# Gate projections of a two-block fp32 transformer: sixteen groups of two tiles over ten pipeline steps, and a second branch with two tiles to a PSUM bank

## The chip, the cores and the metric

One core of one Trainium2 chip. The metric is the device time of one execution in microseconds (us), the median of three runs. One more execution was taken with the hardware profiler; its trace is what is read below.

## The reference

Two transformer blocks on 256 tokens of width 2048, one layer each, all in fp32. The change lies in the second block:

```python
proj = h @ w_in[layer]
qa, ka, va, qb, kb, vb, ga, gb = jnp.split(proj, IN_OFFSETS, axis=-1)
ya = sliding_window_attention(qa, ka, va, sink_logits) @ w_branch_a[layer]
yb = stick_breaking_attention(qb, kb, vb) @ w_branch_b[layer]
merged = jax.nn.sigmoid(ga) * ya + jax.nn.sigmoid(gb) * yb
x = x + merged @ w_out[layer]
x = x + swiglu(rmsnorm_2(x, norm_ffn_g[layer]), w_ffn_in[layer], w_ffn_down[layer])
```

`ga` and `gb` are 2048 columns wide each, so the gate projection is a [256 x 2048] by [2048 x 4096] product. Each attention has 16 heads of 64; its output is 1024 wide, and `w_branch_a`, `w_branch_b` take it to 2048.

## The kernel before

All products are in fp32 precision made of three fp32r products: a weight and an activation are each split in a rounded part `hi` and a rest `lo`, and hi*hi, hi*lo and lo*hi are added in PSUM. Features lie on the partitions, the 256 tokens (`T`) in the free dimension; an output tile is 128 features by 256 tokens, an input tile `kt` likewise. The block's activations stand in `pair[:, kt, 0]` (hi) and `pair[:, kt, 1]` (lo).

**Weights.** They stream from HBM in chunks of 128 x 1024 fp32 (512 KB) into six buffers `raw`. For each chunk ScalarE (ACT) copies it, rounded, into `hi` (L383), VectorE (DVE) writes the rest into `lo` (L396), and TensorE (PE) multiplies. `hi` and `lo` have four slots, so ACT may split chunk c only when PE has used chunk c-4 (`weights_used`). A chunk holds eight blocks of 128 x 128. Each engine works through its own list in the order written; semaphores tie them.

**Two forms of the product.** `features` (L436), the wide form: one matmul of `hi` with both parts of the activation (512 columns, into the two halves of a bank) and one of `lo` with the hi part (256 columns, into the second half). A whole bank holds one tile, and DVE adds the halves later (`sum_out`, L1264). `three` (L446) and the same written out at L2110 to L2114: three matmuls of 256 columns into one half of a bank, so two tiles fit in a bank and nothing is left to add.

**Attention pipeline with gates in it.** Eight head pairs (`PAIRS`) go through both attentions in a software pipeline. In step i PE does `window_scores(i)`, `stick_scores(i)`, `flip_window(i-1)` (transposes), `suffix_sums(i-1)` and `mix(i-2)`, and between them `gate_chunks`, eight chunks per step: group i of the gate projection, four tiles, in two banks (0, 1 or 2, 3), by threes. DVE and ACT have the softmax and the stick-breaking arithmetic of the pairs between their splits of the weight chunks. `mix(n)` waits for `sb_d` of pair n+1, which DVE writes at L1587 from the result of `suffix_sums(n+1)` and signals. DVE takes each finished gate group out of PSUM with two multiplies by `rinv` (L1594).

**After eight steps** the gates are done, but the pipeline is not: two mixes, a flip and a suffix sum are left. PE does them between the four chunks (`bra_chunk`) of the first group of the first branch product. Its input is the attention output: ACT copies the mix from PSUM to `qkb` (L1040), rounds it into `pair` (L1045, `o2_hi`), and DVE writes the rest (L1598, `o2_lo`). These writes into `pair` have to come behind the last gate chunk, which reads it.

**The branches.** `bra` (first) and `brb` (second): four groups of four tiles, four chunks a group, wide form, one tile to a bank, groups taking turns with banks 0-3 and 4-7. Per group DVE adds halves (L1264, four), multiplies by the opened gates (L1614, four), and for `brb` also adds the branches (L1620, four) and writes the rest of the sum (L1625, four), between them ACT the rounded part (L1063, four) into `pair2`. `pair2` feeds `out2`, four groups of eight chunks in the wide form.

Of the kernel before, what the change touches and what calls it, by code (L numbers as in the profile page):

```python
# [125 lines left out]
for _s, _n in (("out", 12), ("up", 88), ("down", 16), ("qa", 8), ("kva", 2), ("qkb", 16),  # L126
               ("bra", 16), ("brb", 16), ("out2", 16), ("up2", 88), ("down2", 16)):
# [4 lines left out]
O2_AT = {7: (0, 1), 8: (2,), 9: (3, 4, 5, 6, 7)}  # L132
# [62 lines left out]
def two_blocks(nc, stream, cvec_d, c_bc_d, vecs_d, xc_d, x_d, rpb, w_fnet, base_tab, rope_tab, dft_tab, na_mask,  # L195
               stick_tab, dist_tab, out_d):
    ctx = ExitStack()
    with ctx:
# [462 lines left out]
        def _(e):  # L661
# [332 lines left out]

            for i in range(PAIRS + 2):
                b = BASE["gates"] + i * CPG + LEAD

                def hi_of(k):
                    if i < PAIRS:
                        split_hi(e, b + k, b + k + 1)  # L1000
                hi_of(0)
                hi_of(1)
# [10 lines left out]
                hi_of(2)  # L1013
# [9 lines left out]
                hi_of(3)  # L1023
# [6 lines left out]
                hi_of(4)  # L1030
                hi_of(5)
# [63 lines left out]
        def _(e):  # L1095
# [427 lines left out]
            e.wait_ge(s_stick, 16)  # L1523
            for i in range(PAIRS + 2):
                b = BASE["gates"] + i * CPG + LEAD

# [29 lines left out]
                lo_of(1)  # L1556
# [6 lines left out]
                lo_of(2)  # L1563
# [12 lines left out]
                lo_of(3)  # L1576
# [6 lines left out]
                lo_of(4)  # L1583
# [4 lines left out]
                lo_of(5)  # L1588
                lo_of(6)
                lo_of(7)  # L1590
                if i < PAIRS:
                    e.wait_ge(weights_used, BASE["gates"] + (i + 1) * CPG)
                    for q in range(2):
                        e.tensor_tensor(gates[:, 4 * i + 2 * q:4 * i + 2 * q + 2, :], by_two(ps[:, 2 * (i % 2) + q, :]),  # L1594
                                        rinv[:, 1, :].unsqueeze(1).to_broadcast([P, 2, T]), ALU.mult).then_inc(gates_raw, 1)
# [815 lines left out]
```

## Time and profile before

| | |
|---|---|
| median of 3 runs | 2693.95 us (2693.45 to 2694.07) |
| the profiled execution | 2695.51 us, span 2693.7 us |
| PE busy | 2622.0 us, 97% |
| DVE busy | 1767.4 us, 66% |
| ACT busy | 1214.9 us, 45% |

The span reaches from the first to the last instruction of the trace; 1.8 us of the profiled execution lie around it. A matmul's busy time counts until its modelled end, so neighbours overlap: how fast PE goes is read from the starts.

### The profile page before, as it was taken

To read this page: it belongs to the slowest core of one execution; us is meant where nothing else is said; L and a number is where in the kernel's file an instruction comes from. 1 tells how busy PE (TensorE), PEld (TensorE's weight loads), DVE (VectorE), ACT (ScalarE), POOL (GpSimd) and SP (SyncE) were. 2 spreads that over 40 slices of the span, in tenths; PEclk is the share of its full clock that TensorE was granted. 3 is DMA by queue.
4 is the path that set the end of the run, shared out by engine and by line. 5 is a ranking of instruction groups with operands and counts; after the bars stand their busy time and mean duration, and the time that the engine had idled before them with its cause. 6 is when DMAs were issued, how large, how long until landed. Compare 5 with 4: busy or idle time off the path is not lost.

```text
span 2693.7 us, 37948 instructions
## 1 busy us (share of the span) xinstructions
PE 2622.0 (97%) x15626; PEld 2259.4 (84%) x15626; DVE 1767.4 (66%) x2474; ACT 1214.9 (45%) x1603; POOL 32.5 (1%) x31
## 2 busy tenths in 40 slices
PE   6899999989999999999999999989999999999999
PEld 3568867878888888888888899977888888888888
DVE  3256876788888877555656555567766666665555
ACT  4342244445555555444433544444544444444443
POOL 2110000000000000000000000000000000000000
PEclk9999999999999999999999999999999999999999
DMA  8877884757777655555555544444565555555553
GB/s 325 295 274 271 298 280 156 244 189 231 239 235 239 223 190 192 188 188 187 190 188 189 174 147 141 134 142 166 178 202 189 188 190 191 190 190 191 191 188 125
DMA packets 151404, 547.26 MB, mean 203 GB/s; under 512 B 16960, under 2 KB 18880, under 8 KB 150464
## 3 DMA queue, kind: packets, MB, share of 16 engines
q1 hardware_dynamic: 148752, 540.35, 60.2%
q10 hardware_dynamic: 2480, 4.49, 0.6%
q8 instruction: 123, 2.02, 0.3%
q14 instruction: 49, 0.40, 0.0%
HBM read 542.68 MB, written 2.10 MB: 202 GB/s over the span
## 4 chain that ended last, share of the span: by engine, by line
PE 93%; DVE 3%; ACT 2%; DMA 1%; issue 1%; SPq 0%; POOL 0%; ACTq 0%; DVEq 0%
PE ps L444 42%; PE ps L443 21%; PE ps L448 3%; PE ps L441 2%; PE ps L449 2%; PE ps L450 2%; PE ps L2110 2%; PE ps L2112 2%; PE ps L2114 2%; PE ps L456 2%; PE ps L455 2%; PE ps L454 2%; DVE lo L396 2%; PE ps L442 1%; PE ps L1654 1%; ACT hi L383 1%
## 5 line engine op out<-in xcount | busy, mean ns | idle before, releaser
L396 DVE TENSOR_TENSOR lo<-raw,hi 128x1024 fp32r<-128x1024 f32 x822 | 1001.8, 1224 | 796.8 <-ACT hi L383 794.5
L383 ACT ACTIVATE hi<-raw 128x1024 fp32r<-128x1024 f32 x822 | 866.8, 1059 | 1082.8 <-PE ps L444 801.2
L444 PE MATMUL ps<-pair,hi 128*128 128x512 f32 x3674 | 1281.6, 392 | 0.0
L443 PE MATMUL ps<-pair,lo 128*128 128x256 f32 x3674 | 1029.7, 280 | 6.2 <-DVE pair L1598 4.2
L444 PEld LDWEIGHTS ps<-pair,hi 128*128 128x128 f32 x3674 | 691.7, 188 | 149.8
L443 PEld LDWEIGHTS ps<-pair,lo 128*128 128x128 f32 x3674 | 691.9, 188 | 9.8 <-issue 4.6
L444 PE MATMUL ps<-hid,hi 128*128 128x512 f32 x1376 | 477.4, 392 | 0.0
L443 PE MATMUL ps<-hid,lo 128*128 128x256 f32 x1376 | 384.6, 280 | 0.0
L444 PEld LDWEIGHTS ps<-hid,hi 128*128 128x128 f32 x1376 | 258.3, 188 | 56.7
L443 PEld LDWEIGHTS ps<-hid,lo 128*128 128x128 f32 x1376 | 258.3, 188 | 0.3
L1264 DVE TENSOR_REDUCE tmp<-ps 128x256 f32<-128x512 f32 x276 | 186.3, 683 | 5.0 <-PE ps L444 4.6
L407 DVE CUSTOM_DVE_ANT_0 raw<-raw,c_bc 128x1024 f32<-128x1024 f32 x128 | 153.2, 1219 | 0.1
L2110 PE MATMUL ps<-pair,hi 128*128 128x256 f32 x512 | 146.9, 287 | 0.0
L2112 PE MATMUL ps<-pair,hi 128*128 128x256 f32 x512 | 143.4, 280 | 0.0
L2114 PE MATMUL ps<-pair,lo 128*128 128x256 f32 x512 | 143.3, 280 | 0.0
L448 PE MATMUL ps<-both,hi 128*128 128x512 f32 (+1 forms) x272 | 104.4, 384 | 18.3 <-DVE lo L396 15.5
L441 PE MATMUL ps<-pair,hi 128*128 128x512 f32 x262 | 98.0, 406 | 15.7 <-DVE lo L396 7.3
L2110 PEld LDWEIGHTS ps<-pair,hi 128*128 128x128 f32 x512 | 96.4, 188 | 4.6 <-issue 3.7
L2112 PEld LDWEIGHTS ps<-pair,hi 128*128 128x128 f32 x512 | 96.4, 188 | 0.0
L2114 PEld LDWEIGHTS ps<-pair,lo 128*128 128x128 f32 x512 | 96.3, 188 | 0.0
L450 PE MATMUL ps<-both,lo 128*128 128x512 f32 (+1 forms) x272 | 95.2, 350 | 0.0
L449 PE MATMUL ps<-both,hi 128*128 128x512 f32 (+1 forms) x272 | 95.2, 350 | 0.0
(310 smaller groups left out, 2330.9 us busy)
## 6 DMA issues: line engine op xcount, KB each, us to landing
raw<-in_stream SPq DMA_DIRECT2D x1014, 512.0 KB, 4.0
xc<-in_xc SPq DMA_DIRECT2D x4, 1024.0 KB, 8.1
x<-in_x ACTq DMA_DIRECT2D x1, 2048.0 KB, 7.8
out<-out_sb SPq DMA_DIRECT2D x8, 256.0 KB, 2.7
c_bc<-in_c_bc SPq DMA_DIRECT2D x1, 1024.0 KB, 7.6
bias<-in_rpb ACTq DMA_DIRECT2D x4, 256.0 KB, 4.6
raw<-in_stream SPq DMA_DIRECT2D x2, 256.0 KB, 3.3
dft<-in_dft_tab ACTq DMA_DIRECT2D x1, 512.0 KB, 5.6
```

The source lines that it names most:

```text
L383: e.activation(hi[:, c % R, :], raw_of(p), ACT.Copy).then_inc(hi_ready, 1)
L396: e.tensor_tensor(lo[:, c % R, :], raw_of(p), hi[:, c % R, :].bitcast(F32), ALU.subtract)\
L407: e.tensor_tensor_reduce(out=raw_of(p), in0=raw_of(p), in1=c_bc[:, (i % 2) * CH:(i % 2 + 1) * CH], scale=1.0, scalar=0.0, op0=ALU.mult, op ...
L441: e.matmul(out, whi, both_, start=True, stop=False)
L443: e.matmul(out[:, T:2 * T], wlo, act[:, 0, :], start=False, stop=False)
L444: return e.matmul(out, whi, both_, start=False, stop=last)
L448: e.matmul(out, whi, ahi, start=first, stop=False, skip_group_check=True)
L449: e.matmul(out, whi, alo, start=False, stop=False, skip_group_check=True)
L1264: e.tensor_reduce(out, ps[:, bank, :].rearrange("p (s t) -> p t s", s=2), AX_X, ALU.add)\
L2110: e.matmul(out, whi[:, w], pair[:, kt, 0, :], start=(kt == 0 and m % 2 == 0), stop=False, skip_group_check=True)
L2112: e.matmul(out, whi[:, w], pair[:, kt, 1, :], start=False, stop=False, skip_group_check=True)
L2114: last = e.matmul(out, wlo[:, w], pair[:, kt, 0, :], start=False, stop=(kt == KT - 1), skip_group_check=True)
```

## The change

The gate projection's 32 tiles are cut into sixteen groups of two instead of eight of four. A chunk holds four input tiles by two output tiles instead of two by four; the number of chunks (64) and the number of 128 x 128 blocks stay. The product is in the wide form, one tile to a bank, two banks a group, groups taking turns with banks 0, 1 and 2, 3. DVE takes a group out with two sums of halves and one multiply by `rinv` (`gate_sums`).

The 64 chunks lie over all ten steps of the pipeline by a table, `GATE_SLOTS`: six per step in steps 0 to 4, seven in steps 5 to 8, six in step 9. Between `suffix_sums` and `mix` there is one chunk where there were two; between `stick_scores` and `flip_window` one, in steps 5 to 8 two, where there were two. `bra_chunk` is gone: the whole first branch comes after the pipeline. Its first four input tiles stand in a place of their own, `oq` (over `qa`, dead by then), and are written while gate chunks still read `pair`; the other six pairs of tiles go into `pair` behind the last gate chunk.

The second branch is done by threes, two tiles to a bank, and DVE multiplies the gates straight from PSUM, 512 elements at a time; the additions, the rounding and the rests are also done two tiles at a time.

```diff
-               ("qa", 2 * CPG), ("kva", CPG), ("qkb", 4 * CPG), ("vb", 2 * CPG), ("gates", 8 * CPG),
+               ("qa", 2 * CPG), ("kva", CPG), ("qkb", 4 * CPG), ("vb", 2 * CPG), ("gates", 4 * KT),
...
-               ("bra", 16), ("brb", 16), ("out2", 16), ("up2", 88), ("down2", 16)):
+               ("gates", 2 * KT), ("bra", 16), ("out2", 16), ("up2", 88), ("down2", 16)):
...
-O2_AT = {7: (0, 1), 8: (2,), 9: (3, 4, 5, 6, 7)}
+GATE_SLOTS = [(2, 1, 1, 1, 1)] * 5 + [(2, 2, 1, 1, 1)] * 4 + [(2, 0, 0, 0, 4)]
+GATE_AT = [[sum(map(sum, GATE_SLOTS[:i])) + sum(GATE_SLOTS[i][:k]) for k in range(6)] for i in range(PAIRS + 2)]
...
+        oq, _ = place("oq", [P, 4, 2, T], F32R, reg)
...
+        def o2_of(kt):
+            return oq[:, kt] if kt < 4 else pair[:, kt]
+
+        def o2_pair(t, part):
+            return oq[:, 2 * t:2 * t + 2, part, :] if t < 2 else pair[:, 2 * t:2 * t + 2, part, :]
...
+            def o2_split(t):
+                e.wait_ge(o2_raw, 2 * (t % 4) + 2)
+                e.activation(o2_pair(t, 0), qkb[:, 2 * t:2 * t + 2, :], ACT.Copy).then_inc(o2_hi, 1)
...
-                for t in O2_AT.get(i, ()):
-                    e.wait_ge(o2_raw, 2 * (t % 4) + 2)
-                    e.activation(pair[:, 2 * t:2 * t + 2, 0, :], qkb[:, 2 * t:2 * t + 2, :], ACT.Copy).then_inc(o2_hi, 1)
+                hi_of(4)
+                if i == PAIRS:
+                    e.wait_ge(sw_scores, 2 * PAIRS)
+                    o2_split(0)
+                    o2_split(1)
+            e.wait_ge(weights_used, BASE["gates"] + 4 * KT)
+            for t in range(2, PAIRS):
+                o2_split(t)
...
-                for m in range(4):
-                    t = 4 * g + m
-                    e.wait_ge(merged, t + 1)
-                    e.activation(pair2[:, t, 0, :], gates[:, t, :], ACT.Copy).then_inc(m_hi, 1)
+                for m in range(2):
+                    t = 4 * g + 2 * m
+                    e.wait_ge(merged, t + 2)
+                    e.activation(pair2[:, t:t + 2, 0, :], gates[:, t:t + 2, :], ACT.Copy).then_inc(m_hi, 2)
...
+            def o2_low(t):
+                e.wait_ge(o2_hi, t + 1)
+                e.tensor_tensor(o2_pair(t, 1), qkb[:, 2 * t:2 * t + 2, :], o2_pair(t, 0).bitcast(F32), ALU.subtract)\
+                    .then_inc(o2_lo, 1)
+
+            def gate_sums(g):
+                e.wait_ge(weights_used, BASE["gates"] + 4 * (g + 1))
+                for m in range(2):
+                    sum_out(2 * (g % 2) + m, gates[:, 2 * g + m, :])
+                e.wait_ge(sums_ready, SUMS["gates"] + 2 * (g + 1))
+                v = gates[:, 2 * g:2 * g + 2, :]
+                e.tensor_tensor(v, v, rinv[:, 1, :].unsqueeze(1).to_broadcast([P, 2, T]), ALU.mult).then_inc(gates_raw, 1)
...
+                    for c in range(LEAD + GATE_AT[i][k], LEAD + GATE_AT[i][k + 1]):
+                        split_lo(e, BASE["gates"] + c, BASE["gates"] + c + 1)
+                        if c % 4 == 3 and c >= 7:
+                            gate_sums((c - 7) // 4)
...
                         e.wait_ge(sb_suffix, i - 1)
                     e.scalar_tensor_tensor(out=sp_[:, i % 2], in0=zb[:, i % 3], scalar=0.0, in1=lnb[:],
                                            op0=ALU.max, op1=ALU.add).then_inc(sb_sp, 1)
-                lo_of(4)
                 if 1 <= i <= PAIRS:
                     n = i - 1
                     e.wait_ge(sb_suffix, i)
...
+            for t in range(2, PAIRS):
+                o2_low(t)
...
+            for g in range(4):
+                b = BASE["brb"] + g * 4
+                split_lo(e, b + LEAD, b + LEAD + 4)
+                e.wait_ge(weights_used, b + 4)
+                e.wait_ge(gate_open, 4 + g + 1)
+                for m in range(2):
+                    v = gates[:, KT + 4 * g + 2 * m:KT + 4 * g + 2 * m + 2, :]
+                    e.tensor_tensor(v, v, by_two(ps[:, 4 + 2 * (g % 2) + m, :]), ALU.mult).then_inc(gated, 2)
+                for m in range(3):
+                    t = 4 * g + 2 * m
+                    if m < 2:
+                        e.wait_ge(gated, KT + t + 2)
+                        e.tensor_tensor(gates[:, t:t + 2, :], gates[:, t:t + 2, :], gates[:, KT + t:KT + t + 2, :], ALU.add)\
+                            .then_inc(merged, 2)
+                    if m:
+                        t -= 2
+                        e.wait_ge(m_hi, t + 2)
+                        e.tensor_tensor(pair2[:, t:t + 2, 1, :], gates[:, t:t + 2, :],
+                                        pair2[:, t:t + 2, 0, :].bitcast(F32), ALU.subtract).then_inc(m_lo, 2)
...
+            def gate_chunks(a, b):
+
                 for ch in range(a, b):
-                    c = BASE["gates"] + g * CPG + ch
+                    g, c = ch // 4, BASE["gates"] + ch
+                    if ch % 4 == 0 and g >= 2:
+                        e.wait_ge(sums_ready, SUMS["gates"] + 2 * (g - 1))
...
+                    for k in range(4):
+                        kt = 4 * (ch % 4) + k
+                        for m in range(2):
+                            last = features(e, 2 * (g % 2) + m, split_view(hi, c, 4, T)[:, k, tok(m)],
+                                            split_view(lo, c, 4, T)[:, k, tok(m)], px(kt), kt == 0, kt == KT - 1)
...
-            for i in range(PAIRS):
-                window_scores(i)
-                gate_chunks(i, 0, 2)
-                stick_scores(i)
-                gate_chunks(i, 2, 4)
-                if i:
+            for i in range(PAIRS + 2):
+                at = GATE_AT[i]
+                if i < PAIRS:
+                    window_scores(i)
+                gate_chunks(at[0], at[1])
+                if i < PAIRS:
+                    stick_scores(i)
+                gate_chunks(at[1], at[2])
+                if 1 <= i <= PAIRS:
                     flip_window(i - 1)
-                gate_chunks(i, 4, 5)
-                if i:
+                gate_chunks(at[2], at[3])
+                if 1 <= i <= PAIRS:
                     suffix_sums(i - 1)
-                gate_chunks(i, 5, 7)
+                gate_chunks(at[3], at[4])
                 if i >= 2:
                     mix(i - 2)
-                gate_chunks(i, 7, 8)
-            flip_window(PAIRS - 1)
-            e.wait_ge(gates_raw, 2 * (PAIRS - 1))
-            bra_chunk(0)
-            suffix_sums(PAIRS - 1)
-            e.wait_ge(gates_raw, 2 * PAIRS)
-            bra_chunk(1)
-            mix(PAIRS - 2)
-            bra_chunk(2)
-            mix(PAIRS - 1)
-            bra_chunk(3)
...
+                gate_chunks(at[4], at[5])
+            e.wait_ge(o2_raw, PAIRS)
             for g in range(4):
-                e.wait_ge(sums_ready, SUMS["out2"] - 4 + 4 * g)
+                if g == 1:
+                    e.wait_ge(sums_ready, SUMS["gates"] + 2 * KT)
+                elif g >= 2:
+                    e.wait_ge(sums_ready, SUMS["bra"] + 4 * (g - 1))
+                b = 4 - 4 * (g % 2)
+                group(e, BASE["bra"] + 4 * g, 4, 2, GW, wide(range(b, b + 4), o2_of),
+                      need=None if g else lambda kt: e.wait_ge(o2_lo, kt // 2 + 1))
+            for g in range(4):
+                if g == 0:
+                    e.wait_ge(sums_ready, SUMS["bra"] + 12)
+                elif g >= 2:
+                    e.wait_ge(gated, KT + 4 * (g - 1))
+
+                def brb_jobs(kt, whi, wlo, first_, last, g=g):
+                    if g == 0:
+                        e.wait_ge(o2_lo, 4 + kt // 2 + 1)
+                    for m in range(4):
+                        r = three(e, half(4 + 2 * (g % 2) + m // 2, m % 2), whi[:, tok(m)], wlo[:, tok(m)],
+                                  pair[:, 8 + kt, 0], pair[:, 8 + kt, 1], first_ and m % 2 == 0, last)
+                    return r
+                group(e, BASE["brb"] + 4 * g, 4, 2, GW, brb_jobs)
+            e.wait_ge(sums_ready, SUMS["bra"] + 16)
+            for g in range(4):
+                if g == 1:
+                    e.wait_ge(gated, 2 * KT)
+                if g:
+                    e.wait_ge(sums_ready, SUMS["out2"] - 4 + 4 * g)
                 b = 4 * (g % 2)
...
+            out[p] = plain(w_in2, i, CPG, {"kva": 1024, "qkb": 1536, "vb": 3584}[s])
+        elif s == "gates":
```

Where instructions stand now. First PE, in steps 8 and 9 and behind. Before, the last transposes (L2159) are followed by the first branch (L441 to L444), and the suffix sums (L2173 to L2176) come after one chunk of it:

```order
L2112 MATMUL ps<-pair,hi 128x256
L2114 MATMUL ps<-pair,lo 128x256
L2159 MATMUL ps<-base,sa 128x128 x6
L441 MATMUL ps<-pair,hi 128x512
L442 MATMUL ps<-pair,lo 128x256
L441 MATMUL ps<-pair,hi 128x512
L442 MATMUL ps<-pair,lo 128x256
```

In the changed kernel the transposes are L2165 and gate chunks surround them (L452, L453, the wide form, from `pair`):

```order
L452 MATMUL ps<-pair,lo 128x256
L453 MATMUL ps<-pair,hi 128x512
L2165 MATMUL ps<-base,sa 128x128 x6
L452 MATMUL ps<-pair,lo 128x256
L453 MATMUL ps<-pair,hi 128x512
```

and the first branch starts, from `oq` (L450, L451), behind the last gate chunk:

```order
L452 MATMUL ps<-pair,lo 128x256
L453 MATMUL ps<-pair,hi 128x512
L450 MATMUL ps<-oq,hi 128x512
L451 MATMUL ps<-oq,lo 128x256
L450 MATMUL ps<-oq,hi 128x512
L451 MATMUL ps<-oq,lo 128x256
```

So both remaining mixes, the flip and the suffix sums stand between gate chunks, and no branch chunk stands among them.

Then DVE in one pipeline step. Before, step 7: the sums' rest `sp_` (L1581), one split, the subtraction that lets a mix go (L1587), three splits and the gate multiplies:

```order
L396 TENSOR_TENSOR lo<-raw,hi 128x1024
L1581 SCALAR_TENSOR_TENSOR sp__107<-zb,lnb 128x768
L396 TENSOR_TENSOR lo<-raw,hi 128x1024
L1587 TENSOR_TENSOR zb<-zb,ps 128x768
L396 TENSOR_TENSOR lo<-raw,hi 128x1024 x3
L1594 TENSOR_TENSOR gates<-ps,rinv 128x512 x2
```

In the changed kernel, a step in which a `gate_sums` (L1276, L1276, L1547) falls ahead of the same work (L1605, L1610 are the old L1581, L1587):

```order
L1276 TENSOR_REDUCE gates<-ps 128x256 x2
L1547 TENSOR_TENSOR gates<-gates,rinv 128x512
L405 TENSOR_TENSOR lo<-raw,hi 128x1024
L1591 TENSOR_TENSOR small<-small 128x4
L1593 RECIPROCAL small<-small 128x4
L1599 TENSOR_SCALAR sa<-sa,small 128x128
L1599 TENSOR_SCALAR sa<-sa,small 128x256
L1599 TENSOR_SCALAR sa<-sa,small 128x128
L1599 TENSOR_SCALAR sa<-sa,small 128x256
L1605 SCALAR_TENSOR_TENSOR sp__108<-zb,lnb 128x768
L1610 TENSOR_TENSOR zb<-zb,ps 128x768
L405 TENSOR_TENSOR lo<-raw,hi 128x1024 x3
```

The subtraction now comes right behind `sp_`, and the group of three for the gates can stand ahead of the softmax scaling (L1591 to L1599).

Last DVE in a group of the second branch. Before, 20 instructions a group with four splits (L396):

```order
L396 TENSOR_TENSOR lo<-raw,hi 128x1024 x4
L1264 TENSOR_REDUCE tmp<-ps 128x256 x4
L1614 TENSOR_TENSOR gates<-gates,tmp 128x256 x4
L1620 TENSOR_TENSOR gates<-gates 128x256 x2
L1625 TENSOR_TENSOR pair_114<-gates,pair_114 128x256
L1620 TENSOR_TENSOR gates<-gates 128x256
L1625 TENSOR_TENSOR pair_114<-gates,pair_114 128x256
L1620 TENSOR_TENSOR gates<-gates 128x256
L1625 TENSOR_TENSOR pair_114<-gates,pair_114 128x256 x2
L396 TENSOR_TENSOR lo<-raw,hi 128x1024 x4
```

In the changed kernel ten, with the splits L405:

```order
L405 TENSOR_TENSOR lo<-raw,hi 128x1024 x4
L1640 TENSOR_TENSOR gates<-gates,ps 128x512 x2
L1645 TENSOR_TENSOR gates<-gates 128x512 x2
L1650 TENSOR_TENSOR pair_115<-gates,pair_115 128x2x256 x2
L405 TENSOR_TENSOR lo<-raw,hi 128x1024 x4
```

The sums are gone and each of the others works on 512 elements.

## Rows read from the trace of the kernel before

**Rows 1.** The page: span, and section 4, the chain that ended last, by engine.

```profile
span 2693.7 us, 37948 instructions
...
PE 93%; DVE 3%; ACT 2%; DMA 1%; issue 1%; SPq 0%; POOL 0%; ACTq 0%; DVEq 0%
```

**Rows 2.** Who waited for whom, PE, 1509 to 1885 us.

```profile
PE ps L441 <- DVE lo L396: 7.3, 4, 2.8
PE ps L443 <- DVE pair L1598: 4.2, 2, 2.2
PE ps L441 <- DVE pair L1598: 3.7, 1, 3.7
PE ps L443 <- DVE lo L396: 2.0, 1, 2.0
```

**Rows 3.** Stretches: length, busy us of PE, PEld, DVE, ACT, POOL; PEclk, DMA, GB/s.

```profile
1508.50:1739.80 231.30, 231.30 (x1963) 223.15 (x1963) 135.87 (x221) 117.20 (x183) 0.00 (x0) 1.00 0.45 148
1744.32:1749.57 5.25, 5.25 (x16) 4.48 (x17) 0.45 (x1) 0.00 (x0) 0.00 (x0) 0.50 0.15 60
1770.97:1773.70 2.73, 2.73 (x9) 2.34 (x9) 2.73 (x3) 2.48 (x3) 0.00 (x0) 0.50 0.59 201
1869.40:1874.00 4.60, 4.60 (x19) 3.97 (x18) 2.47 (x3) 1.35 (x2) 0.00 (x0) 0.63 0.93 287
```

**Rows 4.** Chain in order of time after the last gate chunk: start, us, what.

```profile
1740.06 1.07 ACT hi L383
1741.15 1.23 DVE lo L396
...
1743.57 0.61 DVE pair L1598
1744.32 0.76 PE ps L441
```

**Rows 5.** The same chain in 1645 to 1690 us.

```profile
1651.25 0.43 PE ps L2131 x2
...
1680.96 0.43 PE ps L2131 x2
```

**Rows 6.** Timeline of PE in one gate stretch; starts of two blocks of three matmuls.

```profile
1682.43 0.28 PE L2110 MATMUL ps<-pair,hi 128*128 128x256 f32 x1
...
1687.36 0.28 PE L2110 MATMUL ps<-pair,hi 128*128 128x256 f32 x1
```

**Rows 7.** Timeline of PE: first matmul (L441) of groups of the later stages.

```profile
1783.46 0.40 PE L441 MATMUL ps<-pair,hi 128*128 128x512 f32 x1
...
1816.77 0.39 PE L441 MATMUL ps<-pair,hi 128*128 128x512 f32 x1
...
1829.09 0.47 PE L441 MATMUL ps<-pair,hi 128*128 128x512 f32 x1 [1.06 <-DVE lo L396]
...
1855.18 0.47 PE L441 MATMUL ps<-pair,hi 128*128 128x512 f32 x1 [1.75 <-DVE lo L396]
...
1881.30 0.39 PE L441 MATMUL ps<-pair,hi 128*128 128x512 f32 x1
```

**Rows 8.** Groups by line, 1509 to 1885 us: count, busy us, mean ns, idle before.

```profile
L396 DVE TENSOR_TENSOR lo<-raw,hi 128x1024 fp32r<-128x1024 f32 x105 | 126.9, 1223 | 122.8 <-ACT hi L383 122.7
L383 ACT ACTIVATE hi<-raw 128x1024 fp32r<-128x1024 f32 x106 | 110.4, 1055 | 146.8 <-PE ps L2114 110.2 <-PE ps L444 34.9 <-PE ps L456 1.7
...
L1264 DVE TENSOR_REDUCE tmp<-ps 128x256 f32<-128x512 f32 x33 | 20.5, 680 | 0.0
...
L1614 DVE TENSOR_TENSOR gates<-gates,tmp 128x256 f32<-128x256 f32 x32 | 11.3, 415 | 0.0
L1594 DVE TENSOR_TENSOR gates<-ps,rinv 128x512 f32<-128x512 f32 x16 | 10.2, 681 | 0.0
...
L1587 DVE TENSOR_TENSOR zb<-zb,ps 128x768 f32<-128x768 f32 x8 | 7.6, 948 | 6.9 <-PE ps L2176 6.9
...
L1598 DVE TENSOR_TENSOR pair<-qkb,pair 128x512 fp32r<-128x512 f32 x8 | 5.1, 686 | 10.9 <-ACT pair L1045 10.9
```

More of the change, by code:

```diff
@@ L993, in _ @@
             e.preload_act_table_set("natural_log_exp_and_others")
+            def o2_split(t):
+                e.wait_ge(o2_raw, 2 * (t % 4) + 2)
+                e.activation(o2_pair(t, 0), qkb[:, 2 * t:2 * t + 2, :], ACT.Copy).then_inc(o2_hi, 1)
             for i in range(PAIRS + 2):
[L996 removed]
                 def hi_of(k):
[L999 to L1000 removed]
+                    split_hi(e, BASE["gates"] + LEAD + GATE_AT[i][k], BASE["gates"] + LEAD + GATE_AT[i][k + 1])
                 hi_of(0)
[L1002 removed]
                 if i < PAIRS:
@@ L1587, in _ @@
                     e.tensor_tensor(zb[:, n % 3], zb[:, n % 3], ps[:, 6:8, 0:W3], ALU.subtract).then_inc(sb_d, 1)
[L1588 to L1595, printed above, removed]
@@ new lines, in _ @@
+                lo_of(2)
+                lo_of(3)
+                lo_of(4)
+                if i == PAIRS:
+                    o2_low(0)
+                    o2_low(1)
+            for t in range(2, PAIRS):
+                o2_low(t)
+            for g in range(4):
+                b = BASE["bra"] + g * 4
+                split_lo(e, b + LEAD, b + LEAD + 4)
+                e.wait_ge(weights_used, b + 4)
+                if g:
+                    e.wait_ge(gated, 4 * g)
+                for m in range(4):
+                    sum_out(4 - 4 * (g % 2) + m, tmp[:, m, :])
+                for m in range(4):
+                    t = 4 * g + m
+                    e.wait_ge(sums_ready, SUMS["bra"] + t + 1)
+                    e.wait_ge(gate_open, g + 1)
+                    e.tensor_tensor(gates[:, t, :], gates[:, t, :], tmp[:, m, :], ALU.mult).then_inc(gated, 1)
@@ L2219, in _ @@
-            suffix_sums(PAIRS - 1)
-            e.wait_ge(gates_raw, 2 * PAIRS)
-            bra_chunk(1)
-            mix(PAIRS - 2)
-            bra_chunk(2)
-            mix(PAIRS - 1)
-            bra_chunk(3)
-            for br, stage in enumerate(("bra", "brb")):
-                for g in range(0 if br else 1, 4):
-                    if br or g >= 2:
-                        e.wait_ge(sums_ready, SUMS[stage] + 4 * (g - 1))
-                    def split_mix(kt, br=br, g=g):
-                        if br and g == 0:
-                            e.wait_ge(o2_lo, 4 + kt // 2 + 1)
-                    b = 4 * (g % 2)
-                    group(e, BASE[stage] + 4 * g, 4, 2, GW, wide(range(b, b + 4), lambda kt: pair[:, 8 * br + kt]),
-                          need=split_mix)
@@ new lines, in _ @@
+            for g in range(4):
[6 more added lines that the diff above has]
+                        e.wait_ge(o2_lo, 4 + kt // 2 + 1)
+                    for m in range(4):
+                        r = three(e, half(4 + 2 * (g % 2) + m // 2, m % 2), whi[:, tok(m)], wlo[:, tok(m)],
+                                  pair[:, 8 + kt, 0], pair[:, 8 + kt, 1], first_ and m % 2 == 0, last)
+                    return r
+                group(e, BASE["brb"] + 4 * g, 4, 2, GW, brb_jobs)
@@ L2239, in _ @@
+            e.wait_ge(sums_ready, SUMS["bra"] + 16)
+            for g in range(4):
+                if g == 1:
+                    e.wait_ge(gated, 2 * KT)
+                if g:
+                    e.wait_ge(sums_ready, SUMS["out2"] - 4 + 4 * g)
                 b = 4 * (g % 2)
@@ L2345, in lay_stream @@
             out[p] = plain(qa, i, CPG)
-        elif s in ("kva", "qkb", "vb", "gates"):
-            out[p] = plain(w_in2, i, CPG, {"kva": 1024, "qkb": 1536, "vb": 3584, "gates": 4608}[s])
+        elif s in ("kva", "qkb", "vb"):
+            out[p] = plain(w_in2, i, CPG, {"kva": 1024, "qkb": 1536, "vb": 3584}[s])
+        elif s == "gates":
+            out[p] = rows(w_in2, 4 * (i % 4), 4, (4608 + (i // 4) * T, 4608 + (i // 4 + 1) * T))
         elif s in ("bra", "brb"):
```

76 lines of the change are left out of this document (7 added, 69 removed).

## The prediction

> **What bounds the kernel now.** I read the page's chain first: PE has 93% of it [rows 1], so only what PE does or waits for counts. The stretch that the change touches goes from the first `window_scores` to the end of the first `out2` group, and the next views cut it in three.
>
> From 1508.5 to 1739.8 us, the eight pipeline steps with the gates, PE is busy without a break and at full clock, with DVE busy 135.9 and ACT 117.2 of 231.3 us [rows 3]. A step lasts 29.7 us [rows 5]. Nothing waits here: time comes only from the matmuls themselves.
>
> Behind it PE waits, nine times, 17.2 us in all: 3.7 and 4.2 for `o2_lo` (L1598) in the first branch, 7.3 and 2.0 for the splits [rows 2]. The chain shows how the first wait comes about: the last gate chunk frees a slot, then hi, lo, the gate multiplies and `o2_lo` follow one another until PE starts at 1744.32 [rows 4]. After three of the gaps PE runs at the lower level of its clock, 1.2 GHz: 5.25 us at 0.50, 2.73 us at 0.50, and 4.60 us at a mean of 0.63 [rows 3]. The reader should see there that a gap is paid twice.
>
> The pure pace of the wide form is read where no group waits: from 1783.46 to 1816.77 three groups of 32 pairs of matmuls, 0.347 us a pair [rows 7]. By threes it is (1687.36 - 1682.43) / 14 = 0.352 us a block [rows 6]. Both do the same 768 columns.
>
> What is lost today: from 1739.8 to the third group of the first branch at 1783.46 are 43.7 us [rows 3, 7]. The work in them is eight chunks of 8 x 0.347 = 2.78 us, 22.2 us, and a flip, a suffix sum and two mixes. A step less its 64 gate blocks leaves 29.7 - 22.5 = 7.2 us for two sets of scores, a flip, a suffix sum and one mix [rows 5, 6]; without the scores and with a second mix I put the four at 6 us (an estimate; no less than 5, no more than 7.2). Lost: 43.7 - 28.2 = 15.5 us. From 1816.77 to 1881.30 are 64.5 us [rows 7] with three branch groups of 11.1 and eight chunks of `out2`, 55.5 us. Lost: 9.0 us. Together 24.5.
>
> **The change part by part.**
>
> *The gates' form.* 512 blocks at 0.347 instead of 0.352: -2.6 us. The wide form with only two banks in turn isn't in the rows here; bounds: nothing gained (0.352, the pace by threes, which also stays in a bank for several matmuls) and -2.6. I take -2.6, since the columns are the same and the row for the wide form is nearest.
>
> The Trainium skill (TensorE: Matmul & The Clock Gate, Back-to-back issue gap) gives an isolated matmul at the high clock its columns over 2.4 GHz plus 2.5 ns. By that the wide form would save one such 2.5 ns a block, 1.3 us over the gates, half of what the rows give; by it the whole sum below would be about 1 us smaller. The rows' matmuls are slower than the rule's in both forms, and no run here shows an isolated one.
>
> *The second branch's form.* 128 blocks by threes: 128 x 0.005 = +0.6 us.
>
> *The first branch behind the pipeline.* The wait at the end of the gates is the one to check. After the last gate chunk, at time 0, PE has chunks 0 and 1 of the first branch ready: their input is in `oq`, written in step 8, and their weights are split. Chunk 2 needs `o2_lo` of the third pair at 5.6 us. ACT has hi of one chunk, then the rounding: about 1.9. DVE has lo of that chunk to 2.5 (1.22), `gate_sums` of the last group, three instructions of 0.68 [rows 8], to 4.6, and `o2_lo` 0.69 [rows 8] to 5.2. Margin 0.4 us. The remaining five `o2_lo` come every 0.6 us and are needed every 2.8. DVE is free for the next weight chunk at about 8.1, its lo is there at 9.3, and PE wants it at 11.1: margin 1.8. So this wait goes, and what would be late next is that `o2_lo`, by tenths. Price if all I left out adds up to 1 us: 0.6.
>
> *The remaining mixes, flip and suffix sum.* They stand between gate chunks rather than branch chunks. `mix(6)` in step 8 has the same single chunk behind the suffix sums as every other mix now (below), `mix(7)` the first two chunks of step 9 besides.
>
> *The splits.* Behind its `o2_lo` today DVE comes late to the next weight chunks, and PE waits for them, 2.8 us of the 7.3 [rows 2]. With the margin of 1.8 this goes too.
>
> *Second branch, DVE.* Today a group costs DVE 4 x 1.22 for splits, 4 x 0.68 sums, 4 x 0.415 multiplies [rows 8] and eight more of about 0.42: 12.6 us, more than the 11.1 us of PE: that is the 1.1 and 1.8 us at each group's head [rows 7]. After: 4.9 + six of about 0.68 = 9.0 us against 8 x 4 x 0.352 = 11.3 us of PE. The bound goes back to PE. Into `out2`: PE has four chunks split, 11.1 us; ACT's rounding comes at 4.4 to 5.5, its table load 1.3, hi 1.06, lo 1.22 gives about 9.1. Margin 2. So all 9.0 us of loss go.
>
> *Inside the steps.* This is what has to pay. A step of six chunks lasts 29.7 - 22.5 + 48 x 0.347 = 23.9 us. DVE needs per step: (135.9 - 64 x 1.22 - 16 x 0.68) / 8 = 5.8 for attention [rows 3, 8], 6 x 1.22 = 7.3, and one and a half `gate_sums` of 2.04, 3.1: 16.2 of 23.9 us. ACT: (117.2 - 64 x 1.06) / 8 = 6.2, and 6.3: 12.5. Neither is the bound. Latency is: `mix` now has one chunk, 2.78 us, behind the suffix sums. DVE's subtraction takes 0.95 [rows 8] and I give the hand-over from PE 0.3: margin 1.5 us, if DVE stands free. In front of it in DVE's list stand the scaling and `sp_`, and nothing else. Counting one step through, `sp_` ends 1 us before the suffix sums do. In a step where a `gate_sums` (2.0) stands ahead of these, the subtraction is about 0.9 late, and the margin 0.6 to 0.8. No wait, then; the other steps have more.
>
> *The transfers.* Six chunks of 512 KB in 23.9 us are 132 GB/s, less than today's 148 [rows 3]; the second branch asks 186, less than the 201 of a stretch above [rows 3]. Nothing.
>
> **Sum.** 24.5 lost and given back + 2.6 - 0.6 = 26.5 us. The other way round, the end of the first `out2` group: 1739.8 - 2.6 + 6 + 44.4 (128 pairs) + 45.1 (128 blocks) + 22.2 = 1854.9 against 1881.30 [rows 3, 7], 26.4 us. Behind that point the instructions are the same. I take 0.4 off for hand-overs between kinds of work that have no row and say 26.0. The profiled execution would go from 2695.51 (span 2693.7, rows 1) to 2669.5; it stood 1.6 us above the median of the runs, 2693.95, so the median goes to **2668.0 us**.
>
> **The rivals.**
>
> *Small waits come back.* The margins of 0.4 at `o2_lo` and 0.6 to 1.5 at the mixes are smaller than what I can count. If each of the seven mixes of steps 2 to 8 waits 0.5 to 1 us and `o2_lo` as well, 4 to 8 us are gone: 2672 to 2676. For it: DVE is at 68% in the step. Against: its list has no wait in front of the subtraction that isn't met earlier.
>
> *Only one half works.* If the second branch stays bound by DVE and its list, for instance by the rounding on ACT between two DVE steps, its 9.0 us stay and the clock drop ahead of `out2` with them: 2677. Against: ACT's L1063 steps fall from four to two a group.
>
> *The other side: the pipeline starves.* A shorter step leaves less cover for the chain scores, softmax, flip, mix. It decides from 26 / 9 = 2.9 us of waiting in each of steps 1 to 9, that is when the subtraction comes 1.5 + 2.9 = 4.4 us later than I count. One way there: `gate_sums` and a split both falling ahead of the softmax scaling with the exponentials late by as much. Then 3.5 us a step would make 9 x 3.5 - 26 = +5.5, 2699.5. Against: the chain has 23.9 us a step and ACT half of it free.
>
> *No effect of the form.* If the wide form in two banks goes at the pace of threes, 2.6 us less gain: 2670.6.
>
> **How the numbers follow.** Forecast as worked out, within 2.5 us: 0.70. Form without effect 0.07. Small waits 0.16. Half 0.04. Starving 0.03. The likeliest case's own range is 2666 to 2670.5: 5 to 7.2 us for the four pieces and the hand-overs. For 8 in 10 the upper end goes into the small waits: 2665.5 to 2674. What a measurement of this kernel tells from no change is about 0.2%, 5.4 us. Faster by more 0.96, within 0.01, slower 0.03.
>
> **What would show it.** PE's list of waits between the first scores and `out2` is empty or under 1 us. The granted clock is 1.00 in all of it. Starts of `window_scores` lie 23.9 us apart in steps 1 to 4 and 26.6 in steps 5 to 7. The gate blocks pace at 0.347. Branch groups start every 11.1 and 11.3 us. The first `out2` group ends near 1855. I am wrong if PE waits for DVE's subtraction (the old L1587) at each mix, or if a gap stands at the third chunk of the first branch; and if the clock is below 1 in the steps.

## The result and the profile after

| | before | changed |
|---|---|---|
| median | 2694.01 us (2693.45 to 2695.08, 4 runs) | 2670.07 us (2669.32 to 2671.33, 4 runs) |
| span of the profiled execution | 2693.7 us | 2668.3 us |

The ratio is 0.9911, 95% interval 0.9894 to 0.9928: faster by 0.9%. Forecast were 2668.0 us and a range of 2665.5 to 2674. The changed kernel ran again beside another experiment below with 2670.18 us.

The page's totals and its chain by engine, of the changed kernel:

```profile
span 2668.3 us, 37181 instructions
...
PE 2615.0 (98%) x15242; PEld 2235.9 (84%) x15242; DVE 1776.2 (67%) x2466; ACT 1213.5 (45%) x1595; POOL 32.4 (1%) x31
...
PE 95%; DVE 2%; ACT 1%; DMA 1%; issue 0%; SPq 0%; POOL 0%; ACTq 0%; DVEq 0%
```

DVE has 9 us more work than before and the kernel is shorter. What moved is the chain's share on DVE and ACT, which went to PE [rows 1].

The stretches of the changed kernel, columns as in [rows 3]: the ten steps, the first branch, the second, and the first `out2` group.

```profile
1509.00:1743.70 234.70, 234.70 (x1521) 202.63 (x1521) 157.72 (x255) 120.34 (x189) 0.00 (x0) 1.00 0.43 144
1743.70:1788.10 44.40, 44.40 (x257) 39.09 (x257) 35.48 (x49) 24.96 (x27) 0.00 (x0) 1.00 0.57 184
1788.10:1833.20 45.10, 45.10 (x385) 45.06 (x385) 33.69 (x42) 23.80 (x26) 0.00 (x0) 1.00 0.55 181
1833.20:1855.40 22.20, 22.20 (x130) 19.56 (x129) 13.32 (x14) 10.79 (x11) 0.00 (x0) 1.00 0.66 215
```

PE is busy in all of it and the granted clock is 1.00, 2.4 GHz. The list of PE's waits between 1505 and 1885 us is empty, where before it had 17.2 us in eight waits [rows 2]; the forecast's text counts nine, its sum is right. The branches take 44.4 and 45.1 us, the two terms of the forecast's second sum to the tenth.

From here on one number is compared: the length from the first matmul of `window_scores(0)` to the first of the second `out2` group, "the stretch". Before it ends at 1881.30 [rows 7], and this is its start in the timeline of PE:

```profile
1508.32 0.48 PE L2130 MATMUL ps<-ka,qa 64*128 64x128 f32 x2
```

So it lasted 372.98 us. In the changed kernel its start, the first matmul of the third group of the first branch, and its end:

```profile
1509.06 0.48 PE L2136 MATMUL ps<-ka,qa 64*128 64x128 f32 x2
...
1765.96 0.39 PE L450 MATMUL ps<-oq,hi 128*128 128x512 f32 x1
...
1855.41 0.39 PE L450 MATMUL ps<-pair,hi 128*128 128x512 f32 x1
```

346.35 us, so 26.6 us less; the forecast's two sums gave 26.5 and 26.4. The third group of the first branch, which started at 1783.46 before [rows 7], cuts the stretch in a first part (gates, attention, first branch) and a second (the rest of the first branch, the second branch and the first group of `out2`):

| | first part | second part |
|---|---|---|
| before | 275.14 us | 97.84 us |
| changed | 256.90 us | 89.45 us |
| less by | 18.24 us | 8.39 us |

The whole span fell by 25.4 us only, because the stretch starts 0.74 us later and 0.5 us more came behind it. The code ahead of the stretch is the same in all kernels here, and in the eleven profiles it took 1505.24 to 1509.58 us. So the stretch tells effects of 1 us apart (it came to 346.35 us again in e9 below) and the end-to-end time doesn't.

The steps themselves, the chain in order of time of the changed kernel (L2136 is the first matmul of `window_scores`):

```profile
1598.02 0.41 PE ps L2136 x2
...
1621.81 0.42 PE ps L2136 x2
...
1648.39 0.42 PE ps L2136 x2
```

A step of six chunks takes 23.8 us and one of seven 26.6, where 23.9 and 26.6 were forecast. Step 1, which has no mix, takes 21.9 and not the 23.9 that the forecast names for steps 1 to 4. Before, eight chunks took 29.7 [rows 5].

The form in two banks, which had no row before (timeline of PE, the matmul with `lo` of each pair):

```profile
1683.83 0.28 PE L452 MATMUL ps<-pair,lo 128*128 128x256 f32 x1
...
1687.64 0.28 PE L452 MATMUL ps<-pair,lo 128*128 128x256 f32 x1
```

Eleven pairs in 3.81 us, 0.346 us a pair, against 0.347 with four banks in turn [rows 7]: two banks in turn cost nothing.

The handing over to the first branch, ACT and then DVE of the changed kernel, from two timelines (PE starts the branch at 1743.76):

```profile
1744.02 1.06 ACT L392 ACTIVATE hi<-raw 128x1024 fp32r<-128x1024 f32 x1 [1.71 <-PE ps L453]
1744.99 3.22 ACT L1006 ACTIVATE pair<-qkb 128x512 fp32r<-128x512 f32 x6
```

```profile
1745.12 1.23 DVE L405 TENSOR_TENSOR lo<-raw,hi 128x1024 fp32r<-128x1024 f32 x1 [1.55 <-ACT hi L392]
1746.26 1.28 DVE L1276 TENSOR_REDUCE gates<-ps 128x256 f32<-128x512 f32 x2
1747.58 0.69 DVE L1547 TENSOR_TENSOR gates<-gates,rinv 128x512 f32<-128x512 f32 x1
1748.18 3.69 DVE L1538 TENSOR_TENSOR pair<-qkb,pair 128x512 fp32r<-128x512 f32 x6
```

The first `o2_lo` of the six ends at about 1748.9; PE wants it two chunks after 1743.76, at 1749.3. That is the margin of 0.4 us of the forecast, and it held.

### The profile page after: what moved, and what is told of

Same layout as the page of the kernel before. It is cut to its first block, busy times and chain, and to the rows that moved or that the text cites. A ratio compares the mean times of both kernels' runs of the same rounds, so it can differ in the third digit from the quotient of the medians.

```text
span 2668.3 us, 37181 instructions
## 1 busy us (share of the span) xinstructions
PE 2615.0 (98%) x15242; PEld 2235.9 (84%) x15242; DVE 1776.2 (67%) x2466; ACT 1213.5 (45%) x1595; POOL 32.4 (1%) x31
## 4 chain that ended last, share of the span: by engine, by line
PE 95%; DVE 2%; ACT 1%; DMA 1%; issue 0%; SPq 0%; POOL 0%; ACTq 0%; DVEq 0%
PE ps L453 46%; PE ps L452 24%; PE ps L457 3%; PE ps L458 3%; PE ps L459 3%; PE ps L450 3%; PE ps L465 2%; PE ps L463 2%; PE ps L464 2%; PE ps L451 1%; PE ps L1679 1%; DVE lo L405 1%; DMA raw<-in_stream 1%; PE ps L1890 1%; ACT hi L392 1%; PE ps L1862 1%
## 5 line engine op out<-in xcount | busy, mean ns | idle before, releaser
L405 DVE TENSOR_TENSOR lo<-raw,hi 128x1024 fp32r<-128x1024 f32 x822 | 1001.9, 1224 | 772.9 <-ACT hi L392 770.7
L453 PE MATMUL ps<-pair,hi 128*128 128x512 f32 x3994 | 1391.8, 392 | 0.0
L452 PE MATMUL ps<-pair,lo 128*128 128x256 f32 x3994 | 1120.1, 280 | 0.0
L453 PEld LDWEIGHTS ps<-pair,hi 128*128 128x128 f32 x3994 | 750.5, 188 | 161.5
L452 PEld LDWEIGHTS ps<-pair,lo 128*128 128x128 f32 x3994 | 750.6, 188 | 6.0 <-issue 2.4
L453 PE MATMUL ps<-hid,hi 128*128 128x512 f32 x1376 | 477.4, 392 | 0.0
L452 PE MATMUL ps<-hid,lo 128*128 128x256 f32 x1376 | 384.6, 280 | 0.0
L453 PEld LDWEIGHTS ps<-hid,hi 128*128 128x128 f32 x1376 | 258.3, 188 | 56.7
L452 PEld LDWEIGHTS ps<-hid,lo 128*128 128x128 f32 x1376 | 258.3, 188 | 0.3
L1276 DVE TENSOR_REDUCE tmp<-ps 128x256 f32<-128x512 f32 x260 | 176.4, 683 | 5.0 <-PE ps L453 4.6
L457 PE MATMUL ps<-both,hi 128*128 128x512 f32 (+1 forms) x272 | 104.8, 385 | 18.1 <-DVE lo L405 15.3
L450 PE MATMUL ps<-pair,hi 128*128 128x512 f32 x262 | 96.9, 402 | 4.6 <-DVE pair L605 4.6
L457 PEld LDWEIGHTS ps<-both,hi 128*128 128x128 f32 x272 | 53.2, 196 | 44.6 <-DVE lo L405 20.2
L451 PE MATMUL ps<-pair,lo 128*128 128x256 f32 x262 | 73.9, 282 | 0.0
L1679 PE MATMUL ps<-raw,csil 128*32 128x256 f32 x512 | 45.3, 432 | 19.7 <-DMA raw<-in_stream 16.6
L450 PEld LDWEIGHTS ps<-pair,hi 128*128 128x128 f32 x262 | 49.7, 190 | 15.3 <-issue 6.9
L459 PEld LDWEIGHTS ps<-both,lo 128*128 128x128 f32 x272 | 53.6, 197 | 6.9
L959 ACT ACTIVATE gate<-tmp 128x256 f32<-128x256 f32 x44 | 18.4, 419 | 90.0 <-DVE tmp L1423 90.0
```

The costliest lines, as they stand in the source:

```text
L405: e.tensor_tensor(lo[:, c % R, :], raw_of(p), hi[:, c % R, :].bitcast(F32), ALU.subtract)\
L450: e.matmul(out, whi, both_, start=True, stop=False)
L451: return e.matmul(out[:, T:2 * T], wlo, act[:, 0, :], start=False, stop=False)
L452: e.matmul(out[:, T:2 * T], wlo, act[:, 0, :], start=False, stop=False)
L453: return e.matmul(out, whi, both_, start=False, stop=last)
L457: e.matmul(out, whi, ahi, start=first, stop=False, skip_group_check=True)
```

## The experiments

Times stand beside runs of the kernel before on the same chip, whose medians were 2694.35 (e1 to e4), 2692.92 (e5 to e7) and 2694.7 us (e8, e9). Ratios are to those, with 95% intervals.

### e1: the second branch alone

Edit to the kernel before: PE by threes in banks 0 to 7, two a group, and DVE's list of the changed kernel; in short

```diff
-                    for m in range(4):
-                        sum_out(4 * (g % 2) + m, tmp[:, m, :])
...
+                for m in range(2):
+                    v = gates[:, KT + 4 * g + 2 * m:KT + 4 * g + 2 * m + 2, :]
+                    e.tensor_tensor(v, v, by_two(ps[:, 2 * g + m, :]), ALU.mult).then_inc(gated, 2)
...
+                        r = three(e, half(2 * g + m // 2, m % 2), whi[:, tok(m)], wlo[:, tok(m)],
```

> The kernel before with the second branch alone in the new form (threes, two tiles to a bank, multiplies straight from PSUM, two tiles at a time); gates and pipeline as before. The stretch from the first window scores to the second out2 group was 373.0 us before and is 346.4 in the changed kernel. Theory (DVE with 12.6 us a group was the bound of the second branch): the 9.0 us lost there come back less 0.6 for the form, stretch 364.6, time 2685.5, and the waits in the first branch stay (3.7, 2.0, 2.2, 2.8). Rival (the group heads waited for ACT's rounding and splits, whatever DVE does): at least half of the gaps stay, stretch 368 or more.

2686.55 us, ratio 0.9974 (0.9964 to 0.9984). The stretch is 364.84 us, 8.14 less than before, where 8.4 were expected. PE's waits in it:

```profile
PE ps L443 <- DVE pair L1598: 4.2, 2, 2.2
PE ps L441 <- DVE pair L1598: 3.7, 1, 3.7
PE ps L441 <- DVE lo L396: 2.8, 1, 2.8
```

The reader should set this beside [rows 2]: the three `o2_lo` waits and the one of 2.8 are the same to the tenth, and the other four of the second branch and `out2` (4.5 of the 7.3, and 2.0) are gone. The second part is 89.46 us, that of the changed kernel to 0.01. The rival, that the group heads wait whatever DVE does, is out. But the edit also merges ACT's roundings, two tiles at a time; that DVE's list alone sets the gaps takes e6.

### e6: DVE's work back into the second branch

Edit to the changed kernel, ahead of the two multiplies of each group, in short; the results are not used:

```diff
+                for m in range(NX):
+                    if m % 4 == 0:
+                        e.wait_ge(again, NX * g + m)
+                    e.tensor_reduce(tmp[:, m % 4, :], ps[:, 4 + 2 * (g % 2) + m % 2, :].rearrange("p (s t) -> p t s", s=2), AX_X,
+                                    ALU.add).then_inc(again, 1)
```

with NX = 6.

> The changed kernel with six idle sums of halves of 0.68 us added to DVE's list in each group of the second branch, ahead of its multiplies: DVE at 9.0 + 4.1 = 13.1 us a group against 11.3 us of PE. Their results are not used. Theory (DVE's list was the bound of this stage, not the banks or ACT): PE waits at group heads again, 1.2, 2.0, 2.0 and 2.5 us, stretch 354.0, and with the clock falling ahead of out2 about 1.7 more; time 2677.5 to 2679.5. Rival (what helped was PE's form and two banks a group, with groups no longer waiting for sums): stretch stays under 348.

2677.59 us, ratio 0.9943 (0.9927 to 0.996); the stretch 354.98, 8.6 more than the changed kernel. PE's waits:

```profile
PE ps L459 <- DVE lo L407: 2.9, 2, 1.6
PE ps L452 <- issue: 1.8, 1, 1.8
PE ps L454 <- DVE lo L407: 1.0, 1, 1.0
```

The gaps are back with DVE's work alone, the form and the banks of PE unchanged. They sum to 5.7 us where 7.7 were expected. For the one of 1.8, at the first matmul of `out2` (1837.58 us), the view names no releaser; in DVE's timeline the first split for `out2` starts at 1836.25 and takes 1.2 us, so PE starts as it ends. The other 2.9 of the 8.6 us are what is left, the lower clock and restarts. One row from the stretches has the 3.9 us behind that wait, at a mean granted clock of 0.56:

```profile
1837.58:1841.50 3.92, 3.92 (x14) 3.39 (x15) 3.92 (x5) 1.48 (x2) 0.00 (x0) 0.56 0.73 199
```

### e2: gates by threes

Edit to the changed kernel; ten steps stay, DVE multiplies straight from PSUM.

```diff
-                            last = features(e, 2 * (g % 2) + m, split_view(hi, c, 4, T)[:, k, tok(m)],
...
+                            last = three(e, half(g % 4, m), split_view(hi, c, 4, T)[:, k, tok(m)],
...
-                for m in range(2):
-                    sum_out(2 * (g % 2) + m, gates[:, 2 * g + m, :])
```

> The changed kernel with the gate projection by threes, two tiles to one bank, four banks in turn, and so without DVE's 32 sums of halves; the ten steps and chunks stay. Theory (PE alone sets the steps, the form is worth 0.005 us a block): 512 blocks at 0.352, stretch 346.4 + 2.6 = 349.0, time 2672.7, no waits. Rival (the two forms are equal within 1 us, or DVE's relief of 20 us gives something back): stretch 346.4 or less.

The stretch is 349.22 us, 2.87 more than the changed kernel. No wait of PE. 2670.85 us, ratio 0.9916 (0.9899 to 0.9933): end to end the two can't be told apart, the execution that was profiled having reached the stretch at 1505.58, 3.5 us sooner. DVE is relieved of 32 sums, 22 us, and PE doesn't gain by it.

### e3: eight steps instead of ten

```diff
-GATE_SLOTS = [(2, 1, 1, 1, 1)] * 5 + [(2, 2, 1, 1, 1)] * 4 + [(2, 0, 0, 0, 4)]
+GATE_SLOTS = [(2, 2, 1, 2, 1)] * 8 + [(0, 0, 0, 0, 0)] * 2
```

> The changed kernel with the 64 chunks in the first eight steps, (2, 2, 1, 2, 1) each, none in steps 8 and 9. Theory (what cost time before was the first branch chunks waiting for o2_lo between the mixes; the leftover chain flip, suffix sums, mix by itself costs PE only its own latencies): PE waits about 2.5 us for the subtraction before the seventh mix and twice 0.8 for the copies, stretch about 350.5, up to 352 if the clock falls, time 2674 to 2676. Rival (the spreading over ten steps is what brings the first branch's 15.5 us): stretch 358 to 362.

The stretch is 350.49 us, 4.14 more than with ten steps. The waits inside the pipeline's end, from the timeline of PE (L2204 is a mix):

```profile
1739.86 0.43 PE L2204 MATMUL ps<-saT,va 128*64 128x128 f32 x2 [2.81 <-DVE zb L1610]
1742.39 0.40 PE L2204 MATMUL ps<-saT,va 128*64 128x128 f32 x2 [0.73 <-issue]
```

and 0.7 for the last copy, 4.2 in all; the clock stays at 1.00. End to end 2671.73 us (0.992, 0.9905 to 0.9934), below the 2674 to 2676 expected: the profiled execution started the stretch at 1506.12, 2.9 us sooner than that of the changed kernel. So the ten steps are worth 4.1 us where the first branch's input is early.

### e8: the kernel before with the first branch's first group behind the mixes

```diff
             flip_window(PAIRS - 1)
-            e.wait_ge(gates_raw, 2 * (PAIRS - 1))
-            bra_chunk(0)
             suffix_sums(PAIRS - 1)
-            e.wait_ge(gates_raw, 2 * PAIRS)
-            bra_chunk(1)
             mix(PAIRS - 2)
-            bra_chunk(2)
             mix(PAIRS - 1)
-            bra_chunk(3)
+            e.wait_ge(gates_raw, 2 * (PAIRS - 1))
+            e.wait_ge(gates_raw, 2 * PAIRS)
+            for c in range(4):
+                bra_chunk(c)
```

> The kernel before with one edit on TensorE: the four chunks of the first branch's first group (bra_chunk) come behind the last flip, suffix sums and both mixes instead of between them. Theory (most of the 15.5 us lost there came from chunks whose input hangs on the mixes, three o2_lo waits with the clock falling behind them; without them only the pipeline's own latencies stay): PE waits about 2.8 us for the subtraction and 0.7 for a copy, and no o2_lo; the second branch keeps its gaps; stretch 373.0 - 12.5 = 360.5, at most 362, time 2681.5 to 2683. Rival (the chunks were useful cover and only the gates can take their place): stretch 369 or more.

2682.58 us, ratio 0.9958 (0.9942 to 0.9975); the stretch 360.09, 12.9 less than before. PE's waits in it:

```profile
PE ps L441 <- DVE lo L396: 4.5, 3, 1.8
PE ps L2198 <- DVE zb L1587: 3.3, 1, 3.3
PE ps L443 <- DVE lo L396: 2.0, 1, 2.0
PE ps L2198 <- issue: 0.7, 1, 0.7
```

No `o2_lo` is left among them, nor the wait of 2.8 for a split that followed; the second branch's and `out2`'s four stay (4.5 and 2.0). One move in PE's list, with nothing in the gates changed, gives about half of what the whole change gives. Not all of it comes from the first branch. Its third group starts here:

```profile
1769.13 0.39 PE L441 MATMUL ps<-pair,hi 128*128 128x512 f32 x1
```

The first part is then 263.84 us, 11.3 less than before. The second is 96.25, 1.6 less, though nothing in it was changed and its waits are the same: behind its wait of 2.0 us the clock stayed at 1.00 this time (see the last section). That 1.6 is no effect of the move.

What held the chunks up in the kernel before differs from chunk to chunk. Chunk 0 waited 3.7 us for its input, which may be written only behind the last gate chunk [rows 4]; chunk 1 didn't wait. Chunk 2 waited 2.0 us, in the chain in order of time of the kernel before:

```profile
1756.22 0.60 ACT qkb L1040
1756.82 0.53 ACT pair L1045
1757.37 0.70 DVE pair L1598
1758.21 0.36 PE ps L443
```

The copy (L1040) is that of the seventh mix, `mix(6)`. The input of chunk 2 comes from `mix(4)` and `mix(5)`, copied a step earlier; its rounding (L1045) only stands behind the new copy in ACT's list. Chunk 3 waited 2.2 us for the mix just ahead of it, whose result it needs. So the chunks looked like cover for the attention's chain, but one needed its end and another stood behind a part of it in a list.

### e5 and e7: no early input

Edit to the changed kernel (e5), the same on ACT and DVE:

```diff
-                if i == PAIRS:
-                    e.wait_ge(sw_scores, 2 * PAIRS)
-                    o2_split(0)
-                    o2_split(1)
+            e.wait_ge(sw_scores, 2 * PAIRS)
             e.wait_ge(weights_used, BASE["gates"] + 4 * KT)
-            for t in range(2, PAIRS):
+            for t in range(PAIRS):
                 o2_split(t)
```

and e7 is this with the table of e3.

> The changed kernel with all eight writes of the first branch's input behind the last gate chunk, the two that go into oq too (rounding and o2_lo), so that nothing of it is ready when the gates end. Theory (a margin of 0.4 us at the third chunk with two chunks of 2.8 us ahead): the first chunk now waits for the chain hi, lo, gate sums, o2_lo, about 5.1 us; stretch 346.4 + 5.1 = 351.5, and after a gap of that length the clock falls as before behind 3.7 us, 2.5 us more, 354; time 2677 to 2678. Rival (the weights of the first branch, not its input, are what comes last after the gates): stretch under 349.

2677.31 us, ratio 0.9942 (0.9927 to 0.9957); the stretch 353.59. PE's one wait, in its timeline:

```profile
1747.52 0.76 PE L450 MATMUL ps<-oq,hi 128*128 128x512 f32 x1 [5.08 <-DVE oq L1535]
```

Expected were 5.1, and 2.5 for the clock; the stretch came out 7.24 longer than the changed kernel's. The first matmul takes 0.76 us, as behind the first gap before [rows 4], at the lower clock.

> Eight steps as in e3 and no early input as in e5 together; the first branch whole behind the pipeline. Theory (in e3 the gates are done long before the first branch, so the place of its own for the input gives little there; with the writes listed behind the last copy of a mix only the hand-over copy, rounding, o2_lo is left): PE waits 1.3 us more than in e3, stretch 351.8 to 352.3, time 2673 to 2674. Rival (the early input is worth the same 5 us in any order): stretch 355 or more.

The stretch is 351.80 us, 1.31 more than e3 (wait for `o2_lo` 2.0 in place of the 0.7 for the copy); 2673.6 us, ratio 0.993 (0.9915 to 0.9945). So the early input is worth 7.2 us with the gates over ten steps and 1.3 with eight, where the gates are done long before the first branch. Without it, ten steps (353.59) are slower than eight (351.80): spreading the gates over ten steps pays only together with the early input.

### e4: the mix at once

```diff
+GATE_SLOTS = [(2, 1, 1, 0, 2)] * 5 + [(2, 2, 1, 0, 2)] * 4 + [(2, 0, 0, 0, 4)]
```

> The changed kernel with the chunk between the suffix sums and the mix moved behind the mix in steps 0 to 8: (2, 1, 1, 0, 2) and (2, 2, 1, 0, 2). Theory (the mix has a margin of about 1.6 us, and 0.8 in one step, that the chunk of 2.8 us gives): seven mixes wait 1.1 to 2.0 us each for DVE's subtraction, stretch 355.2, time 2679. If the gaps bring the clock down a few us more. Rival (the subtraction is done long before, the margin is far larger): no wait, stretch 346.4.

2678.03 us, ratio 0.9942 (0.9927 to 0.9957); the stretch 357.03, 10.7 more. Seven waits, 8.5 us; two of them in PE's timeline:

```profile
1672.57 0.43 PE L2204 MATMUL ps<-saT,va 128*64 128x128 f32 x2 [1.05 <-DVE zb L1610]
...
1701.47 0.69 PE L2204 MATMUL ps<-saT,va 128*64 128x128 f32 x2 [2.24 <-DVE zb L1610]
```

The chunk that was taken away lasts 2.78 us. So the changed kernel has a margin of 2.78 - 1.05 = 1.7 us at six of the seven mixes and 2.78 - 2.24 = 0.5 at one, that of step 7, where a `gate_sums` stands right in front of the softmax scaling in DVE's list. DVE shows it: in step 6 the subtraction (L1610) waited for PE's suffix sums, in step 7 it came without idle time behind the work in front.

```profile
1671.56 0.95 DVE L1610 TENSOR_TENSOR zb<-zb,ps 128x768 f32<-128x768 f32 x1 [0.37 <-PE ps L2182]
...
1697.67 0.69 DVE L1547 TENSOR_TENSOR gates<-gates,rinv 128x512 f32<-128x512 f32 x1
...
1700.47 0.94 DVE L1610 TENSOR_TENSOR zb<-zb,ps 128x768 f32<-128x768 f32 x1
```

Behind that wait the clock fell (0.83 in the 10 us after), which is most of the 2.2 us that the waits don't explain.

### e9: the changed kernel again

> The changed kernel again, beside e8 on the same chip. All theories: stretch 346.3 to 346.5, no wait of PE in it, time 2670 plus or minus 1.5.

2670.18 us, ratio 0.9907 (0.9892 to 0.9922). The stretch is 346.35 us again, with no wait.

## Why the prediction was right

**Bound and loss.** PE's chain and PE's waits were read as the place of the time. 24.5 us were called lost. The changed kernel has none of these waits, and the stretch fell by 26.6, in the two parts that the forecast has: 15.5 + 2.6 = 18.1 were due in the first and 18.24 came, 9.0 - 0.6 = 8.4 in the second and 8.39 came.

**The first branch.** 15.5 us were expected back; 18.24 less the 2.87 of the form (e2) are 15.4. e8 gets 11.3 of them by moving four chunks, and e3 has the other 4.1, the ten steps in place of eight. The forecast named the pieces but gave no share to each. The flip, suffix sum and two mixes, an estimate of 6 us, come to 6.1: the 234.70 us up to the branch, less the 231.48 from the stretch's start to the last gate chunk before (1508.32 to 1739.80), plus the form's 2.87.

**The margins.** Forecast were 0.4 us at the third chunk, 1.5 at the mixes and 0.6 to 0.8 in the worst step. The trace and e4 show 0.4, 1.7 and 0.5. None turned into a wait. These are tenths, and the worst one was smaller than forecast. But for the rival of small waits, with 0.5 to 1 us at each of seven mixes, the subtraction would have had to come over 2 us later at six of them.

**The second branch.** 9.0 lost less 0.6 for the form made 8.4; e1 alone has 8.38 in the second part (8.14 in the whole stretch), and e6 shows that it is DVE's list.

**The form.** Of bounds of 0 and 2.6 us the larger was taken; e2 measures 2.87, a little beyond it. The Trainium skill (TensorE: Matmul & The Clock Gate, Back-to-back issue gap) gives a figure for an isolated matmul from which the estimate was 1.3 us; the rows and e2 have double that, and the measurement decides.

**Where it is off.** The forecast took 0.4 us off its sum for hand-overs between kinds of work, and said 26.0; the stretch gave 26.6, so nothing shows that term. The median came out at 2670.07 against 2668.0, 2.1 us too high, for two reasons that lie outside the stretch. First, the forecast took all outside it as unchanged, and in the two profiles it wasn't: +0.74 us ahead and +0.5 behind, so that the profiled execution fell by 25.4. Second, it took 1.6 us off because the profiled execution before stood that far above its median; the one of the changed kernel stood at its median (2670.11 against 2670.07). That is the scatter of single executions, and in the eleven profiles the start of the stretch alone differs by up to 4.3 us. One thing goes with it: between 385 and 396 us the granted clock was 1.00 in the five profiles that reach the stretch by 1506.12 us (e1, e2, e3, e7, e8), and 0.69 to 0.84 in the six that reach it at 1507.57 or later. Whether that makes the difference isn't shown.

## What to carry to other kernels

Filler work between the links of a latency chain helps only if it hangs on the chain neither by its data nor by its place in a list: four chunks, three of which waited, cost 11.3 us more as "cover" than behind the chain, and work that was ready (the gates) covers the same chain without a wait. Count what each engine's list holds between two links, not busy shares: DVE at 67% of the steps left 0.5 us at the tightest mix, and in the second branch, at 12.6 us against 11.1, a few merged instructions were worth 8 us. When effects of 1 to 3 us are asked for, compare a stretch between two fixed instructions of the profile, since end to end they drown.

## What the runs showed of the hardware

The clock doesn't fall behind every gap, and the gap's length doesn't decide it between 1.8 and 3.3 us. Before, a wait of 2.0 us inside the first group of `out2` was followed by 4.6 us at a mean of 0.63 [rows 3]; in e8 the same wait of 2.0 us in the same place was followed by none, and this group took 24.5 us against 26.1. The lower clock also came behind 1.8 us in e6 (0.56 over 3.9 us), 2.2 in e4 (0.83 over 10 us) and 2.8 before (0.50 over 2.7 us [rows 3]). It stayed at 1.00 behind the 2.0 and 2.2 us at the third and fourth chunk of the first branch before, 2.0 in e7, 2.8 in e3 and e7, and 3.3 in e8, whose stretch from 1735 to 1760 us holds that wait (PEclk is the third number from the end):

```profile
1735.00:1760.00 25.00, 20.98 (x162) 18.86 (x161) 12.48 (x16) 15.09 (x20) 0.00 (x0) 1.00 0.28 91
```

Behind the longest gaps here, 3.7 us (before and e1) and 5.1 (e5), it fell each time. Whether a gap of some 2 us is paid twice is therefore worth 1.6 us either way in this place, which no forecast from the gap's length alone could have had.
